# Attention of a hybrid layer step: value products in column halves with sums from the exponentials, and another order around the first scores

## The reference, cut to what matters

```python
z = rms_norm(x, g_mix_norm) @ w_in          # q, latent, key rope, u, gate_a, gate_b
s = q_nope @ k_nope.T + q_rope @ k_rope.T   # per head, a query sees its chunk of 64 and what is before
p = softmax(where(visible, s * scale, -inf))
attn = p @ v
rec = rg_lru(causal_dwconv(u))              # a = exp(log_a); mult = sqrt(1 - a*a); h = a*h + mult*(i*u)
mixed = sigmoid(gate_a) * attn + sigmoid(gate_b) * rec
x = x + mixed @ w_out
x = x + (silu(gate) * val) @ w_down         # gate, val: convolved halves of rms_norm(x) @ w_up
```

## Time and profile before

| | |
|---|---|
| three runs | 874.54, 876.79, 877.03 us, median 876.79 |
| profiled execution | 874.96 us, of which the span of the trace is 872.9 |
| busy in the span | PE 849.6 (97%), weight loads 815.3, DVE 568.0 (65%), ACT 366.7 (42%), POOL 191.6 (22%) |
| granted clock of TensorE | 0.996 over the span |
| chain that ended last | PE 87%, ACT 5%, DVE 4% |
| before the attention | 0 to 156 us |
| pairs 0 to 5 | 156 to 368 us, a steady pair 35.8 us |
| pairs 6 and 7 | 368 to 415 us, without the key and query products of later pairs |
| output, up and down products | 415 us to the end, PE busy throughout |

### The profile page before, as it was taken

The page is one execution under the profiler, slowest core; times in us unless marked ns, Lnnn a source line. Parts: engine busy times, 40 slices in busy tenths (PEclk is TensorE's granted clock), DMA queues, the critical chain, the costliest instruction groups (busy, mean ns, idle before and its releaser), DMA issues.

```text
span 872.9 us, 16689 instructions
## 1 busy us (share of the span) xinstructions
PE 849.6 (97%) x6522; PEld 815.3 (93%) x6522; DVE 568.0 (65%) x998; ACT 366.7 (42%) x609; POOL 191.6 (22%) x206
## 2 busy tenths in 40 slices
PE   5999998899999999999999999999999999999998
PEld 5999998789999889877999999999999999999998
DVE  4586678767675676887656888778777876222121
ACT  6634959655655456657245221222222221122121
POOL 4021122202021121121140333323333234010000
PEclk9999999999999999999999999999999999999999
DMA  8433312031120101100223233232322323233321
GB/s 245 116 90 103 95 49 62 2 80 38 28 52 25 53 25 29 50 1 26 73 75 95 75 94 96 72 96 73 95 82 86 91 71 92 82 105 99 104 56 39
DMA packets 114466, 63.73 MB, mean 73 GB/s; under 512 B 7660, under 2 KB 112878, under 8 KB 114412
## 3 DMA queue, kind: packets, MB, share of 16 engines
q1 hardware_dynamic: 112428, 59.25, 23.7%
q0 software_dynamic: 1936, 3.70, 1.7%
q10 hardware_dynamic: 48, 0.02, 0.0%
HBM read 59.85 MB, written 2.70 MB: 72 GB/s over the span
## 4 chain that ended last, share of the span: by engine, by line
PE 87%; ACT 5%; DVE 4%; issue 2%; DMA 1%; SPq 0%; POOL 0%; ACTq 0%; DVEq 0%; POOLq 0%
PE PS L1605 49%; PE PS L1751 9%; PE PS L1833 6%; PE PS L1767 4%; PE PS L1805 4%; PE PS L1644 3%; PE PS L1710 2%; PE PS L2037 2%; PE PS L1787 2%; PE PS L1742 2%; PE PS L1706 1%; DMA xnat<-in_x_prompt_dram 1%; PE PS L1732 1%; PE PS L1673 1%; PE PS L1812 1%
## 5 line engine op out<-in xcount | busy, mean ns | idle before, releaser
L663 ACT ACTIVATE w_hi<-w_raw 128x1024 fp32r<-128x1024 f32 (+2 forms) x102 | 105.4, 1033 | 315.8 <-PE PS L1605 301.5
L1095 DVE TENSOR_TENSOR w_lo<-w_raw,w_hi 128x1024 fp32r<-128x1024 f32 (+2 forms) x102 | 124.7, 1223 | 117.7 <-ACT w_hi L663 117.5
L1605 PE MATMUL PS<-x2h,w_hi 128*128 128x274 f32 x704 | 147.7, 291 | 0.0
L1605 PE MATMUL PS<-x2h,w_lo 128*128 128x274 f32 x704 | 147.1, 290 | 0.0
L1605 PE MATMUL PS<-x2l,w_hi 128*128 128x274 f32 x704 | 147.1, 290 | 0.0
L1605 PEld LDWEIGHTS PS<-x2l,w_hi 128*128 128x128 f32 x704 | 112.1, 189 | 0.0
L1605 PEld LDWEIGHTS PS<-x2h,w_hi 128*128 128x128 f32 x704 | 112.0, 190 | 0.1
L1605 PEld LDWEIGHTS PS<-x2h,w_lo 128*128 128x128 f32 x704 | 111.4, 189 | 0.0
L625 POOL TENSOR_TENSOR uct<-uct 128x548 f32<-128x548 f32 x22 | 30.1, 1370 | 176.4 <-DVE uct L1558 176.4
L1605 PE MATMUL PS<-hh,w_hi 128*128 128x274 f32 x308 | 64.7, 292 | 0.0
L1605 PE MATMUL PS<-hh,w_lo 128*128 128x274 f32 x308 | 64.6, 291 | 0.0
(11 more groups left out here) (291 smaller groups left out, 1846.3 us busy)
## 6 DMA issues: line engine op xcount, KB each, us to landing
w_raw<-in_w_up_dram SPq DMA_DIRECT2D x44, 512.0 KB, 3.8
w_raw<-in_w_in_dram SPq DMA_DIRECT2D x24, 512.0 KB, 3.8
w_raw<-in_w_down_dram SPq DMA_DIRECT2D x16, 512.0 KB, 4.3
w_raw<-in_w_out_dram SPq DMA_DIRECT2D x8, 512.0 KB, 4.3
w_raw<-in_w_down_dram SPq DMA_DIRECT2D x8, 384.0 KB, 3.9
xnat<-in_x_prompt_dram SPq DMA_DIRECT2D x4, 512.0 KB, 5.2
w_raw<-in_w_in_dram SPq DMA_DIRECT2D x4, 416.0 KB, 7.6
wq<-in_w_q_b_dram SPq DMA_DIRECT2D x8, 192.0 KB, 2.5
```

Of the source, the lines that this page charges most:

```text
L663: nc.scalar.activation(hi[:, slot % 2, 0:n], raw[:, slot % 4, 0:n], ACT.Copy).then_inc(s_hi, 1)
L1095: tt(lo[:, slot % 2, 0:n], raw[:, slot % 4, 0:n], hi[:, slot % 2, 0:n].bitcast(F32), ALU.subtract).then_inc(s_lo, 1)
L1605: last = mm(PS[:, 2 * rank + j, 0:HT], w[:, slot % 2, cols], x[:, k0 + k, j * HT:(j + 1) * HT], start=(k0 + k == 0 and first), stop=(k0 + ...
```

## The change

The scores come in another order: block by block, both heads of a block one after the other, instead of one head's four blocks and then the other's. A value group is made at every second n, for both heads of a block: each product fills 64 columns of the array, head 0 the lower half of bank 3 and head 1 the upper, without the ones. The exponential gives the sum of each row by itself (`accum_out`); DVE inverts two sums at a time, and PE spreads them over the columns through the identity into bank 5. `gated_values` is one pass over both heads, with a second operation that multiplies by the inverse, and stands in the next pair's first step. `head_sums` and `sums_inverse` go; `sums` keeps the sample's 32 columns, and `mix` multiplies only these. A group waits for the gated values of the pair before and for the inverse sums.

Around the first scores, the square roots of blocks 3 to 7 become one row of instructions behind the copies of pair 1's first keys, the split of weight block 12, a gate's tanh and two scans go behind the first scores' work, and the columns of pair 0 follow one scan earlier. Since the square roots now end later, three of their tiles lie in the key columns of pair 1, and SP copies the rotary parts and masks there only when these tiles have been read.

```diff
-        th_at = [v1_at + 2 * TB, None, lru_at + TB, kq_at[1], kq_at[1] + TB, kq_at[1] + 2 * TB]
+        th_at = [v1_at + 2 * TB, None, lru_at + TB] + [kt_at + 2 * NK * 4 + n * TB for n in range(3)]
...
-            return (n % 4 + 1) * P if n < 8 else HP + DEC
+            return (n // 2 + 1) * P if n < 8 else HP + DEC
...
+            sp.wait_ge(s_bt, 6)
+            for s in range(2, 4):
+                sp.dma_start(KT[NOPE:QK, s, :], KT[NOPE:QK, 0, :]).then_inc(s_rope4, 16)
+                sp.dma_start(KT[QK:QK + NT, s, :], c["kmask"]).then_inc(s_mask1, 16)
...
-                    nc.scalar.activation(Pn[:, n % 3, 0:w], bank[:, 0:w], ACT.Exp, bias=sm[:, 2:3]).then_inc(s_e, 1)
+                    nc.scalar.activation(Pn[:, n % 3, 0:w], bank[:, 0:w], ACT.Exp, bias=sm[:, 2:3],
+                                         accum_out=exp_sums(p, n)).then_inc(s_e, 1)
...
                 if p or n >= 2:
-                    act.wait_ge(s_pv, p * 9 + n - 1)
+                    act.wait_ge(s_pv, p * 5 + (n // 2 if n > 1 else n - 1))
...
                     if n == 0 and p == 0:
                         squares_queries(1)
+                        act.wait_ge(s_free, 11)
+                        gate_tanh(gate("A", 1))
...
                     lru_exps(3, 6)
-                    lru_mults(3, 6)
             lru_gates(7)
             lru_exps(6, 8)
-            split_item(I_IN + 12)
-            act.wait_ge(s_free, 11)
-            gate_tanh(gate("A", 1))
             for u in range(4):
                 evacuate_kq(1, u, 4 + u)
-            lru_mults(6, 8)
+            lru_mults(3, 8)
             for u in range(4, 6):
                 evacuate_kq(1, u, u - 4)
+            split_item(I_IN + 12)
...
+            def inverse_of_sums(p, t):
+
+                dve.wait_ge(s_e, 9 * p + 2 * t + 2)
+                c0 = 8 * (p % 2) + 2 * t
+                nc.vector.reciprocal(small[:, 7, 16 + c0:18 + c0], small[:, 7, c0:c0 + 2]).then_inc(s_r, 1)
+
+            def gated_values(p):
+
+                g_p = gate("A", p)[:, 0:SEQ]
                 dve.wait_ge(s_gt, gate_count("A", p))
-                dve.wait_ge(s_pv, 9 * p + 4 * (h + 1))
-                stt(g_p, g_p, 1.0, values_bank(h)[rows(h), :], ALU.add, ALU.mult).then_inc(s_o, 1)
+                dve.wait_ge(s_pv, 5 * p + 4)
+                link(stt(g_p, g_p, 1.0, PS[:, 3, :], ALU.add, ALU.mult))
+                tt(g_p, g_p, PS[:, 5, :], ALU.mult).then_inc(s_ov, 1)
...
+                    if n % 2 and n < 8 and n + p > 1:
+                        inverse_of_sums(p, n // 2)
                     if n < 7:
                         row_max(p, n + 2)
...
                     if n == 0 and p:
                         gated_sample(p - 1)
+                        gated_values(p - 1)
...
             recurrence(3)
-            evacuate_first(11)
-            recurrence(4)
-            dve.wait_ge(s_rope4, 48)
+            dve.wait_ge(s_rope4, 16)
             dve.wait_ge(s_m2, KD)
             columns(0, 0, 4)
             columns(0, 1, 5)
             columns(0, 2, 6)
-            recurrence(5)
             columns(0, 4, 3)
+            recurrence(4)
             row_max(0, 0)
             row_max(0, 1)
+            recurrence(5)
+            split_item(I_IN + 12)
             key_sums(1)
...
             def scores(p, n):
-                h, t = divmod(n, 4)
+                t, h = divmod(n, 2)
...
+            def values(p, t):
+
+                par = p % 2
+                pe.wait_ge(s_ptf, p * 9 + (2 * t + 2))
+                if t == 0:
+                    pe.wait_ge(s_vf, p * 3 + 3)
+                    if p:
+                        pe.wait_ge(s_ov, p)
+                pe.wait_ge(s_r, 4 * p + t + 1)
+                for a in range(t + 1):
+                    for h in range(2):
+                        mm(PS[rows(h), 3, t * P:(t + 1) * P], V[:, par, a, 2 * h, :], PT[:, (h + p) % 2, a * P:(a + 1) * P],
+                           start=(a == 0), stop=(a == t))
+                for h in range(2):
+                    last = mm(PS[rows(h), 5, t * P:(t + 1) * P], inverse_sums(p, 2 * t + h).to_broadcast([P, VD]), ident[:, :],
+                              start=True, stop=True)
+                last.then_inc(s_pv, 1)
...
-                    if n:
-                        values(p, n - 1)
+                    if n and n % 2 == 0:
+                        values(p, n // 2 - 1)
...
             for r in range(3):
                 if r == 1:
                     pe.wait_ge(s_e, 9 * NP_)
-                if r:
-                    pe.wait_ge(s_o, 3 * NP_ - 3 + r)
-                    pe.wait_ge(s_sum, 2 * NP_ - 2 + r)
+                    pe.wait_ge(s_ov, NP_)
```

More of the change, by code:

```diff
@@ L182, in layer @@
         xnl = fixed("xnl", [P, KD, T], F32R)
-        sums = fixed("sums", [P, T])
+        sums = fixed("sums", [P, DEC])
         zone = place
@@ L451, in _ @@
             key_query_weights(2)
+            for t in range(I_IN + 16, I_G + 5):
+                w_in_item(t)
+            sp.wait_ge(s_bt, 6)
+            for s in range(2, 4):
+                sp.dma_start(KT[NOPE:QK, s, :], KT[NOPE:QK, 0, :]).then_inc(s_rope4, 16)
+                sp.dma_start(KT[QK:QK + NT, s, :], c["kmask"]).then_inc(s_mask1, 16)
             sp.wait_ge(s_bt, KD)
@@ L882, in probs_columns @@
                 nc.scalar.activation(PT[:, b, 0:w], PS[:, 6 + b, 0:w], ACT.Copy).then_inc(s_ptf, 1)
-            def head_sums(p, h):
-                act.wait_ge(s_pv, 9 * p + 4 * (h + 1))
-                if h == 0 and p:
-                    act.wait_ge(s_mix, p)
-                nc.scalar.activation(sums[rows(h), 0:SEQ], values_bank(h)[rows(1 - h), :], ACT.Copy).then_inc(s_sum, 1)
             def sample_parts(p):
                 b = p % 2
-                act.wait_ge(s_pv, 9 * p + 9)
+                act.wait_ge(s_pv, 5 * p + 5)
                 nc.scalar.activation(PT[:, b, SP0:SP0 + P], PS[:, 6 + b, SP0:SP0 + P], ACT.Copy).then_inc(s_es, 1)
@@ L907, in columns_left @@
                 act.wait_ge(s_tr, q * 5 + (v + 1))
+                if q == 1 and v == 0:
+                    act.wait_ge(s_bt, 6)
                 if v < 2:
@@ L1328, in gated_sample @@
                     stt(g_p, g_p, 1.0, bank[rows(h), :], ALU.add, ALU.mult)
-                    last = nc.vector.tensor_copy(sums[rows(h), S0:], bank[rows(1 - h), :])
-                last.then_inc(s_o, 1)
+                    last = nc.vector.tensor_copy(sums[rows(h), :], bank[rows(1 - h), :])
+                last.then_inc(s_os, 1)
+                dve.wait_ge(s_os, p + 1)
+                nc.vector.reciprocal(sums[:, :], sums[:, :]).then_inc(s_ri, 1)
             def gated_recurrence(p):
@@ L1387, in attend @@
                     if n == 4:
[L1388 to L1391 removed]
+                        if p == 0:
                             recurrence(6)
@@ L1476, in _ @@
             normalise_queries(0)
-            for q in range(3, 6):
-                lru_input(q)
             gated_input(6)
             evacuate_first(10)
-            split_item(I_IN + 12)
             gated_input(7)
@@ L1783, in transpose_probs @@
                 if n == 1 and p:
-                    pe.wait_ge(s_o, 3 * p)
+                    pe.wait_ge(s_os, p)
                 bank = PS[:, 6 + (n + p) % 2, :]
-                for a in range(n % 4 + 1 if n < 8 else 2):
+                for a in range(n // 2 + 1 if n < 8 else 2):
                     last = nc.tensor.transpose(bank[:, a * P:(a + 1) * P], Pn[:, n % 3, a * P:(a + 1) * P], ident[:, :])
@@ new lines, in sample_parts @@
+            def sample_parts(p):
+                par, b = p % 2, p % 2
+                pe.wait_ge(s_ptf, p * 9 + 9)
+                if p < 2:
+                    pe.wait_ge(s_clear, p + 1)
+                for a in range(3):
+                    for g in range(4 if a < 2 else 2):
+                        tile, h = 4 + a + 2 * (g // 2) if a < 2 else NKT - 1, g % 2
+                        c0 = a * P + g * DEC
+                        last = mm(PS[g * DEC:(g + 1) * DEC, 6 + b, SP0:SP0 + P], PT[:, b, c0:c0 + DEC],
+                                  V[:, par, tile, h:h + 2, :].rearrange("p h n -> p (h n)"),
+                                  start=(a == 0), stop=(a == (1 if g >= 2 else 2)))
```

101 lines of the change are left out of this document (36 added, 65 removed).

## The result

The changed kernel takes 879.03 us (median of 20 runs, 875.42 to 880.04), the kernel before 876.01 (20 runs, 874.24 to 877.26): a ratio of 1.003, interval 1.0022 to 1.0038. That is 3.0 us slower by the medians and 0.30% by the ratio, at the very edge of what was called no change (0.3%, 2.6 us), with an interval that lies wholly on the slower side, and 2.2 us over the named time. The profiled execution took 879.34 us, its span 877.3 against 872.9. One run further down, of the kernel with another order of the halves (1041.67 us, at a granted clock of 0.752 over its span), is left out of that kernel's time.

A forecast was written before the change was run, and what follows sets the result against it. PE's own work was taken to bound the steady pairs; -2.35 + 0.55 + 2.15 - 0.73 + 1.25 = +0.9 made 875.8 profiled, 877.7 by the median; 876.8 was named, own range 873 to 881, whole range 868 to 884.5.

The forecast's parts named there:

- pairs 1 to 4: Steady pairs, counted with pair 5: cheaper value products and two new PE waits make +0.43 us each, +2.15 for pairs 1 to 5.
- the first scores: Start, up to the first gate product: scores come some 4.1 us earlier, of which -2.35 us comes through; bounds -4.1 and 0.
- pair 5: Counted like the steady pairs: value products -0.58, wait at n=2 +0.45, wait at n=3 +0.56, together +0.43 us.
- pair 7: Last pair, few fillers: value products -0.58, wait for first sums +1.05, second output product +0.75, together +1.25 us; bounds 0 and 2.
- Behind the gate product: Pair 0 after its first gate product: more transposes and three later value groups left to do, +0.55 us.
- Value products: Value groups of each pair on PE: products in different column halves run beside each other, 3.85 us a pair, -0.58.
- The wait at n=2: First value group of a pair: PE waits for DVE's chain to the reciprocal of the sums, +0.45 us; bounds 0 and +1.2.
- The wait at n=3: Between key transposes and gate product: the value group there is gone, PE waits for DVE's key columns, +0.56 us; bounds 0.3 and 0.8.
- Pair 6: Second-last pair: a 0.80 wait for DVE goes, value products -0.58, wait at n=2 +0.45, accumulator read +0.2: -0.73 us.
- The first: Rival: the new waits at n=2 and n=3 are absorbed, PE's work alone counts, -7.8 us, 867.2 profiled or 869 median; chance 0.29.
- The second: Rival: DVE's chain ahead of the first value group, pairs 1 to 7, is longer; at +0.75, 881 profiled or 883 median; chance 0.21.
- The third: Rival: the value products' halves don't run beside each other, 6.9 us a pair, 24 us over the forecast, about 900; chance 0.07.

The follow-up runs named there:

- the halves alone: Only values in halves, sums from the exponentials and the block order of the scores, against the kernel before, whose order around the first scores stays: 881.51 us, ratio 1.0063.

## Why the prediction was right or wrong

It named no change, 876.8; the change is +0.3%, with an interval that reaches to both sides of that bound. The time lies inside the forecast's own range, 2.2 us over the named one. The sum told +0.9, and the table without its first row makes +3.2: the largest group of terms, pairs 1 to 4, came out, in part by luck, and three terms were mis-sized, the first scores by 0.9, pair 5 by 0.7 and pair 7 by about 1.

- **The first scores, -2.35: mis-sized.** The two waits of PE shrank as told, and the scores came 4.1 us earlier. The step took the rest of the chain at its old durations and left PE's clock out. Measured -1.46, with the clock at its lower level over the key products, and -3.2 where the clock stays (35.83 against 39.04). Both lie inside the stated bounds, but the clock was no term of them: 0.67 stood in the window from 140 to 145 us of the kernel before, and was not read.
- **Behind the gate product, +0.55:** +0.33 by the fold, and the narrower scores make the fold come 0.41 earlier in pair 1 (0.65 us behind the pair's first row, 1.06 before), so +0.74 by the pair's start. Right.
- **Value products, -0.58 a pair: too large.** The prediction's own numbers, 3.85 for 4.4, make -0.55. Measured, the groups take 3.67 to the next row and about 0.1 each on entering, 4.07 for 4.4 before: -0.33. Halves run beside each other; the error is the changes into and out of the tiles, which cost about 0.25 around each of four groups where 0.2 was told. The rule that the prediction took from the Trainium skill ("TensorE: Matmul & The Clock Gate", Part 3, The mechanism), that weight loads overlap running products only where the row group differs, does not hold here, as it didn't at the quarters: 0.058 us a record, on the same rows.
- **The wait at n=2, +0.45: mis-sized, 0.17.** PE came when told, at S + 5.8 (237.09 and two transposes of 0.11). DVE was 0.3 earlier than told: the sample's part ends at S + 1.89 (233.43), not S + 2.05, and the two gated-values operations take 1.26, not 1.38. Moving the gated values away won exactly this 0.17.
- **The wait at n=3, +0.56: right**, shown by filling it.
- **Pairs 1 to 4, +0.43 each: right as a sum** (+0.42), by two errors that cancel: -0.33 + 0.17 + 0.56 = +0.40.
- **Pair 5, +0.43: wrong, +1.10.** It was counted with the steady pairs. It has no second gate product, so at n=7 the missing value group leaves PE waiting 0.99 for the sample's exponentials, 0.32 before. These 0.67 more and the +0.40 of a steady pair make the +1.10.
- **Pair 6, -0.73: right in size (-0.83), partly by chance, and the step has the wrong split.** The 0.80 went; the wait for ACT grew by 0.67, from 0.87 to 1.54 us, where 0.2 for an accumulator read was told; and no wait stands at n=2, where 0.45 was told (the first group starts 0.32 behind the transposes, 379.66 to 379.98, as in the kernel with the gated values moved). With -0.33 for the value products that makes about -0.5; where the rest comes from was not found. The cause of the longer wait is that of pair 5: the work ahead of it has gone, while the sample's chain over DVE and ACT keeps its length.
- **Pair 7, +1.25: too small, +2.40 with the end by the fold,** +2.1 from the pair's first row, since the fold comes 0.32 earlier in its pair. Waits of 0.51 and 0.26 stand where 1.05 was told, and the second output product costs 0.3 (0.44 behind the fold, 0.14 before), not 0.75. Missing were the sample's exponentials (0.83, before 0.35) and a wait that nothing of before shows: 0.60 for ACT's copy of n=8, which must wait for a group that now reads both buffers. The step looked at the waits that the diff writes down for PE, and cost ACT's new wait at nothing; in the steady pairs that holds, in pair 7 no filler covers it.

None of the rivals happened. The first had both waits absorbed, and one was there in full. The second put its loss at n=2, where the chain was shorter than counted and not longer. The third is refuted by the rows. The loss over the forecast came from the pairs without fillers and from the clock.

The medians move by 1 to 2 us more or less than the traces in four of the kernels (gated values moved, group moved, idle products in the change and in the kernel before). The granted clock of each run is on record, as a mean over its span, and goes with the time. Of the change's 20 runs twelve have 0.992 and take 878.7 to 880.0 us, five 0.994 (877.6 to 878.7), one 0.996 (877.5) and two 0.998 (875.4 and 875.6). With the group at n=3, three of seven have 0.998 (871.4 to 871.8) and one has 0.992 (875.1): about 4 us under the change at the same clock, as in the trace, and the median says more because more of its runs kept the clock. With the gated values moved four of seven have 0.990, which no run of the change has, so the little that this edit wins is lost in the median. In the profiled executions the clock is low in the second 10 us, behind the first scores' waits (1.75 us) and in pair 6 (27.19 us with the halves alone and 27.22 with the group moved, 25.64 in the change), and in some executions not. In which of these places it fell in a run without a profile, what decides it, and the rest of the loss from the idle products in the kernel before stay open.

Of the clock in pair 6, the windows of the change (first) and of the halves alone, behind the same 1.54 us wait:

```profile
395.00:400.00 5.00, 4.49 (x47) 3.55 (x44) 3.76 (x12) 4.28 (x13) 0.00 (x0) 1.00 0.35 107
```

```profile
395.00:400.00 5.00, 5.00 (x51) 4.21 (x50) 3.43 (x6) 2.71 (x8) 0.00 (x0) 0.66 0.35 105
```

## What to carry to other kernels

Where work is grouped to make it cheaper, look at what it used to cover: here the value groups at odd steps filled PE's waits for a copy and for an exponential, and moving one group back behind the transposes was worth 4.2 us by the trace and 5.4 by the median, more than the cheaper products (0.33 in each of eight pairs). Count the stages without fillers (the last pairs) by themselves, each wait anew, and follow a wait that moves to the engine that frees the buffer. And read the granted clock beside each wait: here a wait that was shortened on the path left the work behind the next ones at half speed.

## What the runs showed that was not expected

- The wait and the fall of the clock can be moved apart. 15 idle products in a wait of the kernel before kept the clock there, and the time went up by 0.37%: the lower level came 15 us later, on the chain, which is 0.9 us of it.
- PE starts products of different column halves out of the program's order (260.44 ahead of 260.54), so what was said of the engines at the start, that each works through its instructions in order, doesn't hold for the starts of PE's products. With all of one head first, a pair loses 0.75 us and not the 1.5 to 2.2 that lost neighbours would cost.
